# A decoder step's second layer: the prompt's memory attention placed between its query units, and one chunk moved at the turns

## What is computed

```python
xn = rms_norm(h, norm_mix_pre[l])
proj = xn @ w_in_b[j]                      # 1024 -> 768 + 256 columns
q = proj[..., :SB_WIDTH]                   # queries of the stick-breaking attention
sb_out  = stick_breaking(q, k_all, v_all, sb_bias[j], q_pos, k_pos)
mem_out = memory_attend(proj[..., SB_WIDTH:], mem_k[l], mem_v[l])
mix = concatenate([sb_out, mem_out]) @ w_out_b[j]
h = h + rms_norm(mix, norm_mix_post[l])

def memory_attend(q, mk, mv):
    s = einsum('bthd,bmhd->bhtm', qh, mk) * MEM_DH ** -0.5
    return einsum('bhtm,bmhd->bthd', softmax(s), mv)
```

## Time and profile before

| | us |
|---|---|
| median of 3 runs | 1889.07 |
| lowest, highest | 1888.73, 1897.35 |
| the profiled execution | 1890.35 |
| its span, first to last instruction | 1888.4 |
| PE busy in the span | 1784.3 (94%) |
| DVE busy | 1016.3 (54%) |
| ACT busy | 726.8 (38%) |
| POOL busy | 327.7 (17%) |

### The profile page before, as it was taken

One profiled execution on the slowest core, in us unless ns is written; L12 is line 12 of the kernel. 1 busy time (PEld: TensorE's weight loads), 2 busy tenths in 40 slices (PEclk: granted clock), 3 DMA queues, 4 the chain that ended last, 5 costly groups with the idle time before them and its releaser, 6 DMA issues. The chain is left out here.

```text
span 1888.4 us, 36341 instructions
## 1 busy us (share of the span) xinstructions
PE 1784.3 (94%) x13404; PEld 1644.7 (87%) x13404; DVE 1016.3 (54%) x1848; ACT 726.8 (38%) x1245; POOL 327.7 (17%) x452
## 2 busy tenths in 40 slices
PE   8999899999699999999999999799899999999997
PEld 6999688898498999999998998455588999998997
DVE  3663455552427676666226434565535777768224
ACT  4343333331445333335226113454446333336222
POOL 1554344452001222221000000000000222221000
PEclk9999999998799999999999999899999999999999
DMA  4222111100422222223221216778711222222222
GB/s 170 72 84 78 69 35 34 33 20 21 169 78 68 78 87 79 78 89 106 89 89 65 82 67 258 241 260 267 244 58 54 89 78 88 83 84 76 100 86 87
DMA packets 90655, 188.60 MB, mean 100 GB/s; under 512 B 9442, under 2 KB 41570, under 8 KB 90194
## 3 DMA queue, kind: packets, MB, share of 16 engines
q1 hardware_dynamic: 90050, 185.26, 29.2%
q0 software_dynamic: 528, 2.32, 0.3%
HBM read 176.00 MB, written 11.55 MB: 99 GB/s over the span
## 5 line engine op out<-in xcount | busy, mean ns | idle before, releaser
L673 PE MATMUL PB<-parts,wparts 128*128 128x288 f32 x8664 | 1165.9, 297 | 22.8 <-DVE wparts L642 11.5
L673 PEld LDWEIGHTS PB<-parts,wparts 128*128 128x128 f32 x8664 | 1160.0, 190 | 27.2 <-DVE wparts L642 21.7
L632 ACT ACTIVATE wparts<-ring 128x1024 fp32r<-128x1024 f32 x198 | 209.9, 1060 | 680.0 <-PE PB L673 677.1
L642 DVE TENSOR_TENSOR wparts<-ring,wparts 128x1024 fp32r<-128x1024 f32 x174 | 212.8, 1224 | 270.0 <-ACT wparts L632 260.4
L1032 POOL COPY cnew<-arena 128x2 f32 (+1 forms) x106 | 113.0, 1066 | 340.0 <-DVE arena L957 337.2
L969 DVE SCALAR_TENSOR_TENSOR arena<-arena,ffw 128x512 f32<-128x512 f32 x176 | 133.7, 760 | 19.3 <-DVE arena L970 12.8
L683 PE MATMUL PB<-parts,wparts 128*128 128x288 f32 x648 | 104.8, 310 | 4.5 <-DVE parts L514 3.3
L954 DVE TENSOR_TENSOR arena<-PB,rstd_in 128x288 f32<-128x288 f32 x88 | 40.1, 456 | 121.8 <-PE PB L673 115.2
L683 PEld LDWEIGHTS PB<-parts,wparts 128*128 128x128 f32 x648 | 91.0, 188 | 14.0 <-DVE parts L514 7.3
L1008 DVE SCALAR_TENSOR_TENSOR arena<-arena,dnw 128x512 f32<-128x512 f32 x54 | 58.1, 1075 | 32.8 <-ACT arena L907 27.6
L931 ACT ACTIVATE arena<-arena,ffw 128x512 f32<-128x512 f32 x88 | 63.8, 725 | 27.4 <-issue 15.5
(11 more groups left out here) (309 smaller groups left out, 2076.5 us busy)
## 6 DMA issues: line engine op xcount, KB each, us to landing
ring<-in_w SPq DMA_DIRECT2D x198, 512.0 KB, 3.2
arena<-in_kpages SPq DMA_DIRECT2D x64, 256.0 KB, 5.2
arena<-in_vpages SPq DMA_DIRECT2D x64, 256.0 KB, 4.8
arena<-in_kpages SPq DMA_DIRECT2D x64, 128.0 KB, 2.3
arena<-in_vpages SPq DMA_DIRECT2D x64, 128.0 KB, 2.3
membuf<-in_w SPq DMA_DIRECT2D x8, 512.0 KB, 5.7
arena<-in_state_dn SPq DMA_DIRECT2D x6, 512.0 KB, 5.1
o_dns_s<-arena SPq DMA_DIRECT2D x6, 512.0 KB, 3.9
```

Of the source, the lines that this page charges most:

```text
L632: nc.scalar.activation(wparts[:, 0, k, :], ring[:, k, :], ACT.Copy).then_inc(hi_ready, 1)
L642: nc.vector.tensor_tensor(wparts[:, 1, k, :], ring[:, k, :], wparts[:, 0, k, :].bitcast(F32), ALU.subtract).then_inc(lo_ready, 1)
L673: last = nc.tensor.matmul(dst(b), wparts[:, part, k, block * P:(block + 1) * P], x[:, row_, b * HALF:(b + 1) * HALF], start=start and part ...
```

## The change

The units of `in_b` are taken in another order, the two memory queries first. PE does units 0 to 2, the scores of two prompt chunks, and then lays the steps of the prompt's memory attention between the other units. The samples' part stays behind the last unit. ACT, DVE and POOL are written out in the order that fits, the loop over the units is unrolled, and the prompt chunks use banks 4 to 7 of PSUM, which the units don't use. SP loads the units in the new order; its waits for the samples' memory cache and for the pages are as before. POOL copies the samples' memory queries as soon as both memory units are evacuated.

At the three turns ACT makes the first chunk's high part and square ahead of the high part of the next projection's first weights.

```diff
             act_scaled(act, post, k, 1, dst, 0).then_inc(half_out, 1)
+            if then:
+                act_pre(act, then, post, 0, 0)
             act.wait_ge(unit_done, end - 1)
             if then:
                 act_hi(act, name, 0, 0, UNITS[name])
...
-            for c in range(KD):
+            for c in range(1, KD):
                 act_pre(act, then, post, 0, c)
...
+        def pe_query(pe, u):
+            pe.wait_ge(evacuated, UNIT0["in_b"] + u - 1)
+            pe.wait_ge(lo_ready, SPLIT0["in_b"] + u + 1)
+            for c in range(KD):
+                last = products(pe, "in_b", lambda b: PB[:, 2 * b + u % 2, 0:HALF], u % 2, c, c, c == 0, c == KD - 1)
+            last.then_inc(unit_done, 1)
...
+        def score_bank(layer, t):
+            return 4 * layer + 2 * (t % 2)
+        def turn_bank(layer, t):
+            return 4 + layer * 2 * (t % 2) if t < NCH else 4
+        def out_bank(layer, t):
+            return 4 + 2 * (t % 2) if layer else 6 + t % 2
...
             if layer:
+                for u in range(MEMC + 1):
+                    q_unit(u)
+                pe.wait_ge(evacuated, UNIT0["in_b"] + MEMC)
+                pe.wait_ge(v_read, SBC)
+                scores(0)
+                scores(1)
+                q_unit(3)
+                turn(0)
+                q_unit(4)
+                mixed(0)
+                turn(1)
+                scores(2)
+                q_unit(5)
+                mixed(1)
+                turn(2)
+                scores(3)
+                q_unit(6)
+                mixed(2)
+                turn(3)
+                q_unit(7)
+                mixed(3)
                 pe.wait_ge(evacuated, UNIT0["in_b"] + UNITS["in_b"])
+                sample_scores()
+                turn(NCH)
+                sample_mixed()
+                return
...
@@ def act_mem
+            if layer:
+                for u in range(3):
+                    q_split(u)
+                exped(0)
+                exped(1)
+                q_split(3)
+                copied(0)
+                q_split(4)
+                put(0)
+                copied(1)
+                exped(2)
+                q_split(5)
+                put(1)
+                copied(2)
+                exped(3)
...
@@ def dve_mem
+            if layer:
+                for u in range(MEMC + 1):
+                    q_out(u)
+                maxed(0)
+                maxed(1)
+                scaled(0)
+                scaled(1)
+                q_out(3)
+                q_out(4)
+                maxed(2)
+                scaled(2)
+                q_out(5)
...
-                    pe_split(pe, "in_b")
-                    pe_mem(pe, 1)
+                    pe_mem(pe, 1, lambda u: pe_query(pe, u))
...
+                    pool.wait_ge(evacuated, UNIT0["in_b"] + MEMC)
+                    pool_mem(pool, 1)
                     pool.wait_ge(evacuated, UNIT0["in_b"] + UNITS["in_b"])
                     pool.wait_ge(v_read, SBC)
-                    pool_mem(pool, 1)
                     pool_queries(pool)
...
-            feed("in_b")
+            def query_weights(u, i=0):
+                sp.wait_ge(lo_ready, 2 * i + (SPLIT0["in_b"] + u - 1))
+                r = UNIT0["in_b"] + (u + SBC) % (SBC + MEMC)
+                sp.dma_start(ring[:, u % 2, :], d["w8"][r]).then_inc(w_full[u % 2], 16)
+            for u in range(SBC + MEMC):
+                query_weights(u)
             sp.wait_ge(evacuated, UNIT0["in_b"])
```

More of the change, by code:

```diff
@@ L1610, in scores @@
                 if t >= 2:
-                    pe.wait_ge(m_exped, nth(layer, t - 2))
+                    pe.wait_ge(m_out if layer else m_exped, nth(layer, t - 2))
                 for x in range(4):
                     e, f = x // 2, x % 2
-                    last = nc.tensor.matmul(PB[:, 2 * (t % 2) + e, f * N_MEM:(f + 1) * N_MEM],
+                    last = nc.tensor.matmul(PB[:, score_bank(layer, t) + e, f * N_MEM:(f + 1) * N_MEM],
                                             mq[64 * e:64 * e + 64, f, t * P:(t + 1) * P],
@@ L1632, in turn @@
                 pe.wait_ge(m_scaled, nth(layer, t))
-                if t:
+                if t and not layer:
                     pe.wait_ge(m_copied, nth(layer, t - 1))
+                if t == NCH and layer:
+                    pe.wait_ge(m_out, nth(layer, NCH - 1))
                 for x in range(8 if t < NCH else 4):
-                    last = nc.tensor.transpose(PB[:, 4 + x // 4, (x % 4) * P:(x % 4 + 1) * P],
+                    last = nc.tensor.transpose(PB[:, turn_bank(layer, t) + x // 4, (x % 4) * P:(x % 4 + 1) * P],
                                                prob[t % 2][:, x // 2, (x % 2) * P:(x % 2 + 1) * P], ident)
@@ L1641, in mixed @@
                 pe.wait_ge(m_copied, nth(layer, t))
-                if t >= 2:
+                if t >= 2 and not layer:
                     pe.wait_ge(m_out, nth(layer, t - 2))
@@ L1647, in mixed @@
                     for mc in range(2):
-                        last = nc.tensor.matmul(PB[64 * e:64 * e + 64, 6 + t % 2, f * P:(f + 1) * P],
+                        last = nc.tensor.matmul(PB[64 * e:64 * e + 64, out_bank(layer, t), f * P:(f + 1) * P],
                                                 mv[:, mc, h * DH:(h + 1) * DH], probT[t % 2][:, 2 * x + mc, :],
@@ L1668, in pe_mem @@
             if layer:
-                pe.wait_ge(evacuated, UNIT0["in_b"] + UNITS["in_b"])
-            else:
-                pe.wait_ge(dn_s["dve"].sem, dn_s["dve"].at("oz1"))
+                for u in range(MEMC + 1):
[19 more added lines that the diff above has]
+                mixed(3)
+                pe.wait_ge(evacuated, UNIT0["in_b"] + UNITS["in_b"])
+                sample_scores()
+                turn(NCH)
+                sample_mixed()
+                return
+            pe.wait_ge(dn_s["dve"].sem, dn_s["dve"].at("oz1"))
             scores(0)
@@ L1684, in pe_mem, with act_mem @@
             sample_mixed()
-        def act_mem(act, layer):
+        def act_mem(act, layer, q_split=None):
             def exped(t):
@@ L1692, in exped @@
                 for h in range(4 if t < NCH else 2):
-                    src = (PB[:, 2 * (t % 2) + h // 2, (h % 2) * N_MEM:(h % 2 + 1) * N_MEM] if t < NCH
+                    src = (PB[:, score_bank(layer, t) + h // 2, (h % 2) * N_MEM:(h % 2 + 1) * N_MEM] if t < NCH
                            else PB[:, h, 0:N_MEM])
@@ L1703, in copied @@
                 if t < NCH:
-                    nc.scalar.activation(probT[t % 2][:, :, :], PB[:, 4:6, :].rearrange("p a (x t) -> p (a x) t", t=P),
+                    two = turn_bank(layer, t)
+                    nc.scalar.activation(probT[t % 2][:, :, :], PB[:, two:two + 2, :].rearrange("p a (x t) -> p (a x) t", t=P),
                                          ACT.Copy).then_inc(m_copied, 1)
@@ L1712, in put @@
                 nc.scalar.activation(mixT[:, 6:8, t * P:(t + 1) * P],
[L1713 to L1724, removed]
+                                     PB[:, out_bank(layer, t), 0:2 * P].rearrange("p (f t) -> p f t", f=2), ACT.Copy).then_inc(m_out, 1)
+            if layer:
[13 more added lines that the diff above has]
+                exped(3)
+                put(2)
+                copied(3)
+                put(3)
+                exped(NCH)
+                copied(NCH)
+            else:
+                exped(0)
+                exped(1)
+                for t in range(NCH):
+                    copied(t)
+                    if t:
+                        put(t - 1)
+                    if t + 2 <= NCH:
+                        exped(t + 2)
+                copied(NCH)
+                put(NCH - 1)
             act.wait_ge(m_mixed, nth(layer, NCH))
@@ L1735, in act_mem, with dve_mem @@
             last.then_inc(m_out, 1)
-        def dve_mem(dve, layer):
+        def dve_mem(dve, layer, q_out=None):
             def maxed(t):
@@ L1743, in maxed @@
                 if t < NCH:
[L1744 removed]
+                    nc.vector.tensor_reduce(vmax[t % 2], PB[:, score_bank(layer, t):score_bank(layer, t) + 2, :].rearrange("p a (e m) -> p (a e) m", e=2),
                                             AX_X, ALU.max, negate=True).then_inc(m_maxed, 1)
@@ L1756, in scaled @@
                                         ALU.mult).then_inc(m_scaled, 1)
+            if layer:
[10 more added lines that the diff above has]
+                q_out(5)
+                maxed(3)
+                scaled(3)
+                q_out(6)
+                q_out(7)
+                maxed(NCH)
+                scaled(NCH)
+                return
             maxed(0)
@@ L1764, in pool_mem @@
         def pool_mem(pool, layer):
[L1765 to L1768, removed]
             for h in range(4):
@@ L2167, in pool_queries @@
         def pool_queries(pool):
+            for e in range(2):
+                last = nc.gpsimd.tensor_copy(qblk[64 * e:64 * e + 64, :, :, 8 * e:8 * e + 8],
```

(15 more changed lines are left out.)

2 lines of the change are left out of this document (1 added, 1 removed).

## The result

The changed kernel takes 1902.17 us, the median of 7 runs (1900.22 to 1906.57), against 1889.9 for the kernel before in the same runs (1888.18 to 1897.35). The ratio is 1.0059, 95% interval 1.0046 to 1.0072: 8.7 to 13.6 us slower, 11.2 in the middle. The forecast was 11.8 us slower, 1900.9.

The account below looks back on a forecast made before the run. PE was taken to set the pace nearly everywhere, with no room in the query units. Inserted attention 12.6, tail 0.3 and turns -1.1 summed to +11.8 us on 1889.07: 1900.9 us, range 1896.8 to 1904.4.

Parts of the forecast that it names:

- The insertion: Query units: attention steps laid between them delay the last unit by their full PE time, 12.6 us (11.7 to 14).
- the return to a unit: Query units: seven returns from attention steps at 0.3 us each, 2 us at most, taken only into the upper bound.
- ACT and DVE keep up: Query units: ACT and DVE finish their work in time, waits costed at 0; any exposed one would cost 1 to 2 us.
- the rival of the hidden insertion: Query units: bubbles on PE absorb the inserted steps, time 1888.3, or 1885.2 with the tail at full clock; chance 0.07.
- The tail: Behind the last query unit: samples mixed at 24.3 us instead of 23.96, a loss of 0.3; ends -2.8 and +2.2.
- The load: Samples' memory cache, issued after the last query unit: usable 13.84 us later, whatever PE does meanwhile.
- the half-clock terms: Samples' scores, turn and mixed behind the load: at 1.2 GHz they cost 0.9 + 0.6 + 1.8 = 3.3 us more.
- the upper end only: Tail's worst case: half clock also stretches the first set's 32 matmuls, a loss of 2.2 us.
- The first rival: Tail: PE returns to 2.4 GHz within the first scores, the gain of 2.8 stands, time 1897.8; chance 0.15.
- The turns: At out_a, out_b and down0: ACT's earlier first chunk saves 1.1 us in sum, bounds -1.3 and 0.
- The sign of the middle one: At down0: ACT's weights end 0.1 us later, a small loss where both out turns gain 0.6 each.
- the sum: Whole kernel: 12.6 + 0.3 - 1.1 = +11.8 us on the median 1889.07, giving 1900.9.

Follow-up runs that it names:

- Order alone: Changed kernel with memory queries first and units unrolled, but all the attention behind the last unit as before: ratio to before 0.9996 (0.9982 to 1.0011).
- two chunks: Changed kernel with only prompt chunks 0 and 1 between the units, chunks 2 and 3 behind the last unit: ratio to before 1.0045 (1.0029 to 1.0061).
- the changed kernel with the early pages: Changed kernel with the samples' cache's second half moved half a page slot, fourth page granule issued before the samples' mixed wait: ratio to before 1.0058.
- The pair without the load: Changed kernel and kernel before, each without layer B's loads of the samples' memory cache: ratios to before 1.0034 and 1.0007.
- turns-only: Kernel before with only the edit at the three turns (ACT makes the first chunk ahead of the weights): ratio to before 0.9996 (0.9982 to 1.0011).

## Why the prediction was right, point by point

**The insertion** was forecast at 12.6 us and measured at 13.19. The steps themselves were right: 2.03 + 0.80 + 3.61 + 3.61 + 2.36 = 12.41 us, each from the start of a step (or of two or three in a row) to the start of the unit behind it in the timeline after. Undersized was the return to a unit: the five units that follow an attention step take 6.49 to 6.59 us to the next step and not 6.40, 0.78 together, which I had put at 0 with 2 as the upper bound. That ACT and DVE keep up held: PE waits for nobody there. Order alone and two chunks show the cause: 0, 7.24 and 13.19 us for none, two and four chunks inserted.

The query units gave no slack, so the rival of the hidden insertion falls by the full 13.19. The Trainium skill (Perfetto Trace Analysis, section Optimization Strategy) has it that interleaving may help where the most-contended engine changes from one regime to the next. That condition does not hold here, both regimes needed PE, so the trace neither bears the rule out nor speaks against it.

**The tail** was forecast at a loss of 0.3 and came out 0.11 longer. The load came as worked out, 13.62 for 13.84. Scores, turn and mixed took 1.96, 1.12 and some 3.3 us, near the half-clock terms (the turn 0.1 below its term, mixed 0.5 below, since the clock rose in its second part); the samples were mixed at 23.48, not 24.3. What I took for the upper end only, half clock in the set, came in part: its last 8 matmuls took 1.93 instead of 1.06, so the set's end followed the mixed product by 8.20 and not by 7.6. That the end was forecast to 0.2 is luck: mixed came 0.8 too soon, the set took 0.6 too long. The first rival, full clock at once, falls with these rows. The point itself scatters: mixed came at 23.48 here and at 24.04 in the changed kernel with the early pages, whose steps up to there are the same but for the place of the cache's second half. The pair without the load shows the step on which all rests, 9.4 us against 0.6. It agrees with the rule of the Trainium skill (DMA: Bandwidth & Descriptors, section Rules for kernel authors) on issuing a transfer early with the work between issue and wait: the change kept the issue and moved the work ahead of it.

**The turns** were forecast at -1.1 and measured at -0.61, +0.07 and -0.62, together -1.16. The sign of the middle one came from the same reading: with no late square and scaling between, DVE's split already followed at once.

**What the sum lacked**: +0.53 in stick-breaking attention and +0.35 behind it. The first head's scores run at half clock in the execution after (8 matmuls in 4.63 us, 2.42 before), and PE's next step comes 1.5 us later; 1 us of it is made up by the end of `out_b`. I had followed the clock only to the first set. It is not shown to belong to the change: the turns-only and the order-alone kernel, whose tails are as before, have the same half clock there (4.30 and 4.43 us). What sets it in one execution and not in another stays open. Both differences are within the scatter of their stretches.

So each part of +11.8 was right to 0.6 us, and together they measured 12.1; with the unedited stretches it is the 13.0 of the table. Against the ratio's 11.2 (8.7 to 13.6) it cannot be told more finely.

## What to carry to other kernels

Before laying work from a stage with gaps into a stage without, see what else that work was covering. Here the gaps were cheap, because 13.8 us of a load ran beneath them; moving the work paid its full price in the dense stage and left the load bare. The test is one kernel that drops the load on each side: if it is worth 0.6 us before and 9.4 after, the work belonged where it stood. Whether the load could have been issued earlier, together with the moved work, was not tried: its buffers are in use until the last query unit is done. A stage is dense if an insertion of known size lengthens it by that size, which the trace often shows already in a neighbouring stage.

## What had not been expected of the hardware

Filling a wait with idle transposes does not keep PE at 2.4 GHz through the chain behind it: after 3.50 us of them and 1.09 of scores, waits of 2.81 and 0.69 us, with 0.66 of transposes at full clock between them, stood ahead of a product at half speed (1.93 us for 16 matmuls, against 1.07 in the order-alone kernel). The split-product unit behind an inserted step also takes 0.1 to 0.2 us more than 6.40 (6.49 to 6.59), beyond the step's own time.
